# Block by block: the last output products, the second norm and its tiles in the two layers of a fused two-block kernel

## The reference, cut to what matters

```
for l in range(2):
    h = rmsnorm(x, norm1[l]); p = h @ w_in[l]
    u, q, k, v = split(p)
    y_f = real(fft2(u)) @ w_fourier[l] + b_fourier[l]          # 512 wide
    y_a = windowed_gqa(rope(rmsnorm(q)), rope(rmsnorm(k)), v, sink[l])   # 512 wide
    mix = concat([rmsnorm(y_f, g_fourier_out), rmsnorm(y_a, g_attn_out)])
    x = x + mix @ w_o[l]                     # output products, 1024 x 1024
    h = rmsnorm(x, norm2[l])                 # the second norm
    up = dwconv(h @ w_up[l]) + conv_b        # 1024 x 5632
    x = x + (silu(gate) * val) @ w_down[l]
```

## Time and profile before

| | |
|---|---|
| median of 3 runs | 1504.35 us (1503.44 to 1505.59) |
| the profiled execution's own time | 1506.46 us |
| its span in the profile | 1504.3 us |
| instructions | 18539 |
| busy: PE, DVE, ACT | 1338.0, 1073.6, 598.5 us |

### The profile page before, as it was taken

How to read it: one execution, slowest core, us unless ns; L and a number is a source line. 1 busy time by engine, 2 the same in 40 slices (tenths; PEclk the granted TensorE clock), 3 DMA queues, 4 the chain that set the end, 5 groups by cost and what they waited for, 6 DMA issues and landing times.

```text
span 1504.3 us, 18539 instructions
## 1 busy us (share of the span) xinstructions
PE 1338.0 (89%) x6164; PEld 918.8 (61%) x6164; DVE 1073.6 (71%) x2251; ACT 598.5 (40%) x1222; POOL 276.2 (18%) x263
## 2 busy tenths in 40 slices
PE   7998899988697979789797798989999999899998
PEld 2786664434243435344343346679999876799987
DVE  4598846666767676676767757877887477788864
ACT  5343741322222221212222214565665455656652
POOL 0000002263334444444444420000000000000000
PEclk9999999999898989989898899999999999999999
DMA  9623436799999999999999996433554444244540
GB/s 396 248 112 150 187 135 283 301 423 421 421 422 422 422 422 422 422 422 422 422 421 422 421 420 234 156 145 119 190 201 170 150 142 159 112 169 176 201 156 28
DMA packets 49844, 416.18 MB, mean 277 GB/s; under 512 B 5488, under 2 KB 5616, under 8 KB 7024
## 3 DMA queue, kind: packets, MB, share of 16 engines
q0 software_dynamic: 36864, 268.45, 43.0%
q1 hardware_dynamic: 12912, 146.82, 25.7%
HBM read 414.20 MB, written 1.05 MB: 276 GB/s over the span
## 4 chain that ended last, share of the span: by engine, by line
PE 55%; DMA 17%; DVE 13%; issue 8%; POOL 4%; ACT 2%; POOLq 0%; DVEq 0%; ACTq 0%; SPq 0%
DMA arena<-in_uv,ids 15%; PE ps L1081 9%; PE ps L1333 6%; PE ps L1332 6%; PE ps L1334 6%; PE ps L1146 4%; PE ps L1148 4%; PE ps L1147 4%; POOL arena L733 2%; PE ps L936 2%; DMA ring<-in_b1w 2%; POOL ring L733 2%; DVE ring L2036 2%; PE ps L866 2%; PE ps L867 2%
## 5 line engine op out<-in xcount | busy, mean ns | idle before, releaser
L1081 PE MATMUL ps<-ring,arena 128*128 128x512 f32 x512 | 257.2, 666 | 94.0 <-ACT arena L1544 94.0
L1081 PEld LDWEIGHTS ps<-ring,arena 128*128 128x128 f32 x512 | 108.3, 215 | 238.3 <-issue 132.4
L2036 DVE CUSTOM_DVE_ANT_0 arena<-arena 128x1024 f32<-128x1024 f32 x128 | 156.6, 1226 | 123.7 <-DMA arena<-in_uv,ids 123.7
L1081 PE MATMUL ps<-arena 128*128 128x512 f32 x512 | 225.2, 597 | 4.3 <-ACT arena L1544 4.3
L564 DVE TENSOR_TENSOR arena_r<-ring,arena_r 128x1024 fp32r<-128x1024 f32 x152 | 185.0, 1223 | 58.0 <-ACT arena_r L549 57.5
L1332 PE MATMUL ps<-hH,arena_r 128*128 128x256 f32 x704 | 199.4, 283 | 0.0
L1333 PE MATMUL ps<-arena_r 128*128 128x256 f32 x704 | 199.2, 283 | 0.0
L1334 PE MATMUL ps<-hH,arena_r 128*128 128x256 f32 x704 | 199.2, 283 | 0.0
L733 POOL DMA_INDIRECT ring<-in_uv,ids x128 | 144.5, 1129 | 285.7 <-PE ps L1081 238.5
L733 POOL DMA_INDIRECT arena<-in_uv,ids x128 | 131.1, 1024 | 315.2 <-issue 256.1
L549 ACT ACTIVATE arena_r<-ring 128x1024 fp32r<-128x1024 f32 x152 | 158.9, 1053 | 58.9 <-PE ps L1148 58.6
(11 more groups left out here) (315 smaller groups left out, 1989.5 us busy)
## 6 DMA issues: line engine op xcount, KB each, us to landing
ring<-in_lw SPq DMA_DIRECT2D x39, 2048.0 KB, 7.7
ring<-in_b1w SPq DMA_DIRECT2D x18, 2048.0 KB, 8.8
wqb<-in_wq SPq DMA_DIRECT2D x8, 1024.0 KB, 9.1
ring<-in_lw SPq DMA_DIRECT2D x8, 1024.0 KB, 5.0
ring<-in_lw SPq DMA_DIRECT2D x2, 1088.0 KB, 11.3
arena<-in_uv,ids POOLq DMA_INDIRECT x128, 24.6
ring<-in_uv,ids POOLq DMA_INDIRECT x128, 22.3
cst<-in_const SPq DMA_DIRECT2D x1, 1487.5 KB, 19.1
```

The source lines that it names most:

```text
L1081: last = nc.tensor.matmul(ps[:, 4 + 2 * c + b, :], diag[:, k % 4, :], vrows[at[k]][:, b * 512:(b + 1) * 512], start=False, stop=(close and ...
L2036: V.tensor_tensor_reduce(out=urows[at], in0=urows[at], in1=hrow[:, c, :], scale=1.0, scalar=0.0, op0=ALU.mult, op1=ALU.add, accum_out=dots ...
```

## The change

The output products 5, 6 and 7 of block 0 come before all products of block 1. Piece P_O+7 gets buffers of its own, in memory that is free once the last values are computed; the three shared pairs go on past it. The norms of the mixer, the additions to `xr`, the second norm, its diagonal, the scaled tiles and their parts are done first for block 0 and then for block 1. The tiles of 128 x 256 become two of 128 x 128, in other banks. Of the squares for the second norm, block 0's stay on ACT, block 1's are half on ACT and half on DVE. A `mix_square` and the table switch are moved ahead on ACT.

```diff
 def high_of(l, p):
-    return first_wH[p] if p < 2 else wH[(l * (PL - 2) + p - 2) % PIECES]
+    return first_wH[p] if p < 2 else own_wH if p == P_OWN else wH[buffer_of(l, p)]
 def buffers_free(act, l, p):
-    if p >= 2 + PIECES:
-        act.wait_ge(piece_used, l * PL + p - PIECES + 1)
+    if p == P_OWN:
+        act.wait_ge(l_pv, l * 8 + 8)
+    elif p >= 2 + PIECES:
+        act.wait_ge(piece_used, l * PL + p - PIECES + (0 if P_OWN < p <= P_OWN + PIECES else 1))
...
+def block_tile(c, k):
+    if c == 0:
+        return ps[:, (0, 2)[k // 4], (k % 4) * P:(k % 4 + 1) * P]
+    at = 0 if k < 4 else k % 2
+    return ps[:, (3, 1, 7, 6, 4, 4, 5, 5)[k], at * P:(at + 1) * P]
+def block_high(act, l, c, tiles):
+    for k in tiles:
+        act.wait_ge(l2_tile, l * 8 + block_full(c, k)[0])
+        nc.scalar.activation(hH[:, k, c * P:(c + 1) * P], block_tile(c, k), ACT.Copy, scale=gain[:, k:k + 1])\
+            .then_inc(l2_hi, 1)
+def block_rest(dve, l, c, tiles):     # the low parts, on DVE, after l2_hi
...
 # PE
-                mix_products(5, (0,))
+                mix_products(5, (0,)).then_inc(mix_first, 1)
+                mix_products(6, (0,))
+                mix_products(7, (0,)).then_inc(mix_first, 1)
                 pe.wait_ge(mix_lo, l * 4 + 4)
-                mix_products(4, (1,))
-                mix_products(5, (1,))
-                mix_products(6)
-                mix_products(7)
-                pe.wait_ge(l_rows, l + 1)
-                scaled_tiles()
+                for i in range(4, 8):
+                    mix_products(i, (1,))
+                scaled_tiles(0)
+                scaled_tiles(1)
...
-                                pe.wait_ge(lo_out, l * S_TILES + S_NORM2 + k + 1)
+                                pe.wait_ge(l2_lo, l * 2 * KD + KD + k + 1)
 # ACT
                     if m == 6:
                         mix_high(act, l, 2)
-                chain.run(mix_square(0, 1))
+                        mix_square(0, 1).then_inc(sq_done, 1)
+                table(ACT.Sqrt)
+                roots(2, l * 6 + 9)
                 weight_high(act, l, P_O + 6)
                 mix_high(act, l, 3)
+                weight_high(act, l, P_O + 7)
                 mix_square(1, 1).then_inc(sq_done, 1)
-                table(ACT.Sqrt)
-                roots(4, l * 4 + 9)
-                weight_high(act, l, *range(P_O + 7, P_UP + 2))
+                roots(2, l * 6 + 10, 2)
+                weight_high(act, l, P_UP)
+                act.wait_ge(l_oo, 4 * l + 2)
+                nc.scalar.activation(junk_2[0], xr[:, 0, :], ACT.Square, accum_out=ss[:, 4:5]).then_inc(sq_done, 1)
                 act.wait_ge(l_oo, 4 * l + 3)
-                squares(xr, ss, 0, 1)
-                act.sem_inc(sq_done, 1)
-                roots(2, l * 4 + 10)
+                nc.scalar.activation(junk_2[1], xr[:, 1, 0:512], ACT.Square, accum_out=ss[:, 6:7]).then_inc(sq_done, 1)
+                roots(1, l * 6 + 11, 4)
+                weight_high(act, l, P_UP + 1)
+                block_high(act, l, 0, range(4))
+                roots(1, l * 6 + 12, 5)
+                block_high(act, l, 0, range(4, KD))
+                block_high(act, l, 1, range(KD))
                 table(ACT.Silu)
-                tiles_high(act, l, S_NORM2, hH, lpv(l, "n2"))
                 weight_high(act, l, P_UP + 2)
 # DVE
+                dve.wait_ge(sq_done, l * 6 + 8)
+                variance(2, FW)
                 lrows(7)
                 weight_rest(dve, l, P_O + 6)
                 mix_rest(dve, l, 3)
-                dve.wait_ge(sq_done, l * 4 + 8)
-                variance(4, FW)
-                newton(4, l * 4 + 9)
-                mixed(0, 0)
+                newton(2, l * 6 + 9)
+                mixed(0, 0, 0)
+                mixed(0, 1, 0)
                 weight_rest(dve, l, P_O + 7)
-                mixed(0, 1)
-                dve.wait_ge(l_fo, 4 * l + 4)
-                mixed(1, 0)
-                mixed(1, 1)
+                mixed(1, 0, 0)
+                dve.wait_ge(sq_done, l * 6 + 9)
+                variance(2, FW, 2)
+                mixed(1, 1, 0)
+                newton(2, l * 6 + 10, 2)
+                mixed(0, 0, 1)
+                mixed(0, 1, 1)
+                dve.wait_ge(sq_done, l * 6 + 10)
+                variance(1, D, 4)
+                mixed(1, 0, 1)
+                scale_rows(0, l * 6 + 11, 4)          # newton(1), then the diagonal of block 0
+                weight_rest(dve, l, P_UP)
+                dve.wait_ge(sq_done, l * 6 + 11)
+                run(V.tensor_scalar(mean[:, 6:7], ss[:, 6:7], 1.0 / D, EPS, ALU.mult, ALU.add))
+                mixed(1, 1, 1)
                 dve.wait_ge(l_oo, 4 * l + 4)
-                statistics(l * 4 + 8)
-                # both diagonals
-                weight_rest(dve, l, P_UP)
-                tiles_rest(dve, l, S_NORM2, hL, hH, lpv(l, "n2"), range(4))
+                run(V.tensor_tensor_reduce(out=junk_2[2], in0=xr[:, 1, 512:1024], ...accum_out=ss[:, 7:8]))
+                run(V.scalar_tensor_tensor(mean[:, 5:6], ss[:, 7:8], 1.0 / D, mean[:, 6:7], ALU.mult, ALU.add))
+                V.reciprocal(inv[:, 5:6], mean[:, 5:6]).then_inc(var_ready, 1)
+                block_rest(dve, l, 0, range(2))
+                scale_rows(1, l * 6 + 12, 5)
+                block_rest(dve, l, 0, range(2, KD))
                 weight_rest(dve, l, P_UP + 1)
-                tiles_rest(dve, l, S_NORM2, hL, hH, lpv(l, "n2"), range(4, KD))
+                block_rest(dve, l, 1, range(KD))
                 weight_rest(dve, l, P_UP + 2)
```

More of the change, by code:

```diff
@@ L79 @@
 assert PL % PIECES == 0
-S_NORM1, S_NORM2 = 0, 8
-S_TILES = 16
+S_TILES = 8
+P_OWN = P_O + 7
 MIX_TILES = ((0, 0, 5), (0, 1, 3), (1, 0, 5), (1, 1, 5))
@@ L576, in tiles_rest @@
-        def tiles_rest(dve, l, g0, dst, high, gain, tiles=range(KD)):
+                act.wait_ge(stile_done, l * S_TILES + k + 1)
+                nc.scalar.activation(dst[:, k, :], stile(k), ACT.Copy, scale=gain[:, k:k + 1]).then_inc(hi_out, 1)
+        def tiles_rest(dve, l, dst, high, gain, tiles=range(KD)):
             for k in tiles:
-                dve.wait_ge(hi_out, l * S_TILES + g0 + k + 1)
-                nc.vector.scalar_tensor_tensor(dst[:, k, :], stile(g0, k), gain[:, k:k + 1],
+                dve.wait_ge(hi_out, l * S_TILES + k + 1)
+                nc.vector.scalar_tensor_tensor(dst[:, k, :], stile(k), gain[:, k:k + 1],
@@ new lines, in block_high @@
+        def block_high(act, l, c, tiles):
+            gain = lpv(l, "n2")
+            for k in tiles:
[3 more added lines that the diff above has]
+        def block_rest(dve, l, c, tiles):
+            gain = lpv(l, "n2")
+            for k in tiles:
+                dve.wait_ge(l2_hi, l * 2 * KD + block_full(c, k)[1])
+                nc.vector.scalar_tensor_tensor(hL[:, k, c * P:(c + 1) * P], block_tile(c, k), gain[:, k:k + 1],
+                                               hH[:, k, c * P:(c + 1) * P].bitcast(F32), ALU.mult, ALU.subtract)\
+                    .then_inc(l2_lo, 1)
@@ L1152, in products, with rows_by @@
                     return last
-                def rows_by(p0, w, banks, high, rest, g0=None, only=None):
+                def rows_by(p0, w, banks, high, rest, fresh=False, only=None):
                     kp = PIECE // w
                     for q in only or range(KD // kp):
-                        if g0 is not None:
-                            pe.wait_ge(lo_out, l * S_TILES + g0 + (q + 1) * kp)
+                        if fresh:
+                            pe.wait_ge(lo_out, l * S_TILES + (q + 1) * kp)
                         products(p0 + q, [
@@ L1277, in mix_products @@
                     bank = MIX_BANK[half][n]
-                    products(P_O + i, [
+                    return products(P_O + i, [
                         (ps[:, bank + c, :], mixH[:, 4 * half + 2 * q + kk, c * P:(c + 1) * P],
@@ L1370, in squares, with roots @@
                     chain.run(ins)
-            def roots(n, call):
+            def roots(n, call, at=0):
                 act.wait_ge(var_ready, call)
-                nc.scalar.activation(root[:, 0:n], inv[:, 0:n], ACT.Sqrt).then_inc(root_done, 1)
+                nc.scalar.activation(root[:, at:at + n], inv[:, at:at + n], ACT.Sqrt).then_inc(root_done, 1)
             def mod_row_out(i, bank):
@@ L1584, in _ @@
                     act.sem_inc(sq_done, 1)
[L1585 removed]
+                tiles_high(act, l, hH, lpv(l, "n1"), range(4, KD))
                 weight_high(act, l, 3)
[L1587 removed]
+                roots(2 if l else 4, l * 6 + 7)
                 weight_high(act, l, 4)
```

103 lines of the change are left out of this document (59 added, 44 removed).

## The result

The changed kernel takes 1513.55 us (median of 4 runs, 1512.26 to 1515.23) against 1503.92 beside it: a ratio of 1.0056 with a 95% interval of 1.0040 to 1.0071, between 6.0 and 10.7 us. The medians lie 9.6 us apart; the ratio itself stands for 8.4. It is slower, as forecast (1512.8 us). The profiled execution took 1515.23 us with a span of 1513.4.

What follows compares the result with a forecast made beforehand. The prediction took DVE's list to set the end of the stage between last output product and up loop. 2 x 3.5 + 1.4 = 8.4 us on 1504.35 gave 1512.8 us, range 1507.0 to 1517.5.

Steps and rivals of the forecast that it cites:

- the sum: Whole forecast: up loop 3.5 us later in each of two layers, plus 1.4 for the clock, 8.4 us in all.
- Step A: Block 0's mixer square, moved into the attention loop on ACT, delays PE's last transpose and last values by 0.74 us.
- Step B: Table switch and first roots ahead of P_O+6 on ACT make its parts late; PE waits 0.8 us for it.
- Step C: PE idles 2.6 us at product 7 of block 0, waiting for DVE's low part of P_O+7; last product 4.3 us later.
- Step D: DVE's list from there through norms, diagonals and half tiles: up loop starts 3.5 us later per layer.
- DVE's work alone: Check without any waits: 13.6 us of DVE work to block 1's first low part; stage still ends 0.5 us later.
- The clock: PE's clock falls behind the hole before product 7 of block 0, in one layer of two: +1.4 us in all.
- R3: Rival: clock falls in both layers and also slows the up loop's start; 11.8 us more, 1516 us; chance 23%.
- 0.74 + 0.2 + 0.8 + 2.6: Terms of the last output product's 4.3 us delay on PE, from the moved square through the wait for P_O+7.
- R1: Rival: overlap works, up loop starts at 1019 to 1020.5, some 3 us gained per layer, 1498 us; chance 3%.

Runs made afterwards that it cites:

- e2: Changed kernel with 16 idle identity transposes on PE ahead of product 7 of block 0, filling its wait; 1511.72 us, ratio 1.0037.
- e8: The changed kernel run and profiled once more, nothing altered; 1512.95 us, ratio 1.0051 to the kernel before.
- e1: Changed kernel with DVE's low part of P_O+7 moved ahead of the Newton step and two additions; 1508.85 us, ratio 1.0023.
- e4: Kernel before with only PE's new order (products 5 to 7 of block 0 first) and P_O+7's own buffers; 1516.97 us, ratio 1.0079.
- e3: Changed kernel with the early mixer square, table switch and first roots moved back on ACT, block 0's variance later on DVE; 1517.74 us, ratio 1.0081.
- e5: Changed kernel with P_O+7's parts right after P_O+6's, mixer norms at once, P_UP and P_UP+1 low parts behind the tiles; 1502.95 us, ratio 0.9980.
- e6: e5 with block 1's second half square on ACT too, P_UP's low part meanwhile, roots ahead of other ACT work; 1500.09 us, ratio 0.9970.
- e7: e5 with the second norm's roots, Newton step and both diagonals at once behind the last addition; 1506.86 us, ratio 1.0006.

## Why the prediction was right, point by point

**Direction and size.** Forecast +8.4, measured +9.6 (6.0 to 10.7 by the interval), and +7.0 (5.9 to 9.5) when run again. In the traces: 4.26 and 4.63 us on the stretch per layer (4.10 and 3.33 in the second profile). With the clock's part taken out it is 2.80 and 3.34 (e2), 3.33 in the layer where the clock held, against 3.5 in the sum.

**Step A.** 0.74 forecast; the square takes 0.62 between 995.75 and 996.37 on ACT (the read-out overlaps there). Product 4 of block 0 starts 0.63 us later than before. What it costs in the end is under "What A and B cost".

**Step B.** A wait of 0.8 for P_O+6; measured 0.54 in the first layer, and none in the second, where PE came later itself. The roots wait for DVE's variance only 0.30 us.

**Step C.** A hole of 2.6; measured 2.37 and 2.09, with DVE's list in exactly the order counted (tile, Newton step, two additions, low part). The last product, counted from the start of the stretch: 16.66 before, 22.22 and 22.54 after, +5.6 and +5.9; forecast 4.3 plus the clock's part of it, which the sum put on the chain and not on the last product. At full clock the 4.3 was close: +3.9 in the second layer of e8, +4.3 in both layers with the hole filled. e1 and e4 show that this hole is the main cause.

**Step D.** The waits for the diagonals: 1.4 and 3 forecast, 1.14 and 2.53 measured in the first layer, 0.82 and 2.53 in the second. The square of block 0 was late for P_UP's buffer, as told: ACT waits 3.58 us for PE before L557. A low part of 128 x 128 comes every 0.28 us (eight take 2.24), taken at 0.27. Behind the last product's end the up loop follows after 8.95 us (9.5 forecast, 10.25 before), and that is no gain, as told. The sixteen tile records that follow the second wait took 3.47 us at the lower clock (3.4 forecast) and 2.05 with it at 1.00 (e2).

**DVE's work alone.** The 13.6 us of the check of step D do not follow from its terms, which add up to 14.1; the trace has 13.4 from the same addition to the end of block 1's first low part, its three waits of 1.78, 1.32 and 0.88 left out. The waits are worth 4.0 there, not 3.1.

**The clock.** Here the forecast was too kind: one layer of two was to see a fall among the products, and three of the four in the two profiles of the changed kernel did. In the second layer of the first profile it fell even before the hole, behind two pauses of 0.73 us; step A brings the first of them, the second is there before the change (0.73 us ahead of the last values in both kernels). Windows of the changed kernel there:

```profile
1292.00:1294.00 2.00, 1.27 (x9) 0.81 (x8) 1.32 (x4) 1.40 (x7) 0.00 (x0) 1.00 0.00 0
1294.00:1296.00 2.00, 1.27 (x12) 1.16 (x12) 0.49 (x3) 1.84 (x4) 0.00 (x0) 1.00 0.00 0
1296.00:1298.00 2.00, 2.00 (x10) 1.81 (x10) 1.97 (x6) 1.68 (x4) 0.00 (x0) 0.56 0.06 12
```

The price per fall, 1.4, was right: 1.46 and 1.29 by e2, 1.34 between the two layers of e8. A fall ahead of the hole costs less: PE comes to P_O+7 0.3 us later (14.2 us behind the start of the stretch in place of 13.9). The result cannot tell one fall from two, since a fall is worth less than the 2.6 us between the two measurements. R3, which had the fall in both layers, was nearer in mechanism for the first profile; its further 1.0 per layer for a slow start of the up loop is too much, and shows in one layer of each profile (the first up product lasts 0.55 us; in the first profile the rest of the span is 0.6 us longer than before).

**What A and B cost.** The prediction wrote the late last product as "0.74 + 0.2 + 0.8 + 2.6". The end time was right, for it came from following the lists. But the terms cannot be taken off one by one: e3 takes A and B away and loses 4.8 us, since P_O+7's low part is what PE waits for, and in e3 that stands behind a Newton step that waits for the later roots. The low part stands 4.0 us behind P_O+6's on DVE, and P_O+6's is itself late by A and B: DVE turns from it to the tile 9.74 us behind the start of the stretch, 7.85 before, and runs on from there without a wait. Move it ahead of the Newton step, as e1 does, and the first three terms are a price after all: the last product is 1.82 us late, against 1.74 of them.

**R1** stood at 3% and is what e5 and e6 show to be possible with other lists: they reach its start of the up loop (1020.7 and 1019.9 in the first layer, put on the clock of the kernel before; 1019 to 1020.5 forecast). Merging the mixer's norm (a Newton step and a variance less), and letting P_UP+1's low part wait until block 1's tiles are done, cut DVE's work counted as above from 13.4 to 11.3 us, moving a square to ACT to 10.5. The point that R1 gave, under 10, was not reached and was not needed. As a forecast of this change R1 was rightly small.

## What to carry to other kernels

When products are reordered so that one operand is needed sooner, the operand's producers have to move up on every engine's list; look for the piece that the new order reads first and write down where it stands on the slowest list. A saving in the middle of a queue is not a price: only what the bottleneck waits for last is, and taking away an earlier delay can even lose time. A wait of the matmul engine can cost more than its length, by the clock that falls behind it; filling the wait with idle products bought that part back (1.3 to 1.5 us here), but not the wait. And one profile of a kernel is not enough to say whether the clock falls: two profiles of the same one differed in it.

## What the runs showed of the hardware that I had not expected

The fall of PE's clock after a pause outlives it: after 2.37 us of waiting ten products ran at 0.55 of 2.4 GHz for 3.7 us. With sixteen transposes into an unused bank, and a wait of 0.36 us behind them, it stayed at 1.00. But the same wait of 2.37 us in the second profile of the same kernel was followed by 1.00 too, so the fall is not certain.

Shorter pauses can come before a fall too. The changed kernel, e1 and e2 have two pauses of 0.7 us there, one ahead of the last head's transposes and one ahead of its values. With the second profile of the changed kernel these are eight layers: in four of them the clock fell behind the pauses and in four it did not. The others have only the second pause (the kernel before, e3 to e7): none of their twelve layers shows a fall there. What decides between the four and the four no run shows.

The start of the stretch differs between executions of kernels that do the same work until there: in the first layer the tile that opens the stretch started between 991.87 (e1) and 995.90 us (e5) in the ten profiles. That is 4.0 us in single profiles, as much as most effects here; only the stretch and the intervals over several runs tell the versions apart.
